# Finer first pieces, alternating and limited transfers, and rotary tables spread on chip, at the head of an encoder block

## The reference

```python
h = rms_norm(x, norm_gain[l])                       # over 2048 channels
proj = jnp.einsum('bsd,dc->bsc', h, w_in[l])        # to 11776 columns
qa, ka, va, ga, qb, kb, vb, gb, za, zb = jnp.split(proj, split_at, axis=-1)
# mixer A: 8 query heads, 2 key/value heads of 128, 2-D axial rotary over a grid of 64 columns
qa = axial_rotary(rms_norm(qa, q_norm_gain[l]), row_id, col_id)
ka = axial_rotary(rms_norm(ka, k_norm_gain[l]), row_id, col_id)
ya = grid_gqa_attention(qa, ka, va) * jax.nn.silu(ga)
# mixer B: 3 groups of 4 heads with dilated windows; then both branches are projected,
# gated by sigmoid(za), sigmoid(zb), merged, projected by w_out and added to x; final rms_norm
```

## Time and profile before

| what | value |
|---|---|
| time, median of 3 | 1177.59 us (1177.51 to 1177.87) |
| profiled execution | 1174.25 us |
| its span, slowest core (2) | 1172.4 us (cores: 1166.3 to 1172.4) |
| PE busy | 1125.9 us, 96% |
| DVE, ACT busy | 608.5, 507.4 us |
| moved by DMA | 102.18 MB |

### The profile page before, as it was taken

How to read it: one execution, slowest core, us unless ns; L and a number is a source line. 1 busy time by engine, 2 the same in 40 slices (tenths; PEclk the granted TensorE clock), 3 DMA queues, 4 the chain that set the end, 5 groups by cost and what they waited for, 6 DMA issues and landing times.

```text
span 1172.4 us, 17560 instructions; the slowest of 8 cores (1166.3 to 1172.4 us)
## 1 busy us (share of the span) xinstructions
PE 1125.9 (96%) x5844; PEld 556.0 (47%) x5956; DVE 608.5 (52%) x942; ACT 507.4 (43%) x907; POOL 79.2 (7%) x163
## 2 busy tenths in 40 slices
PE   3899999999999999999999999999999999999996
PEld 1655544444444544544554455444444444444443
DVE  2589878888886555663754654421212122122155
ACT  3465688888886444543543543411111111111232
POOL 0000000000000000000000000011111111010000
PEclk9999999999999999999999999999999999999999
DMA  9956512222232424333323420155656645449433
GB/s 221 261 183 158 106 19 37 37 37 37 37 73 38 89 37 72 55 55 55 57 53 55 70 36 1 19 95 89 117 88 115 103 69 87 70 93 247 129 144 144
DMA packets 30040, 102.18 MB, mean 87 GB/s; under 512 B 3456, under 2 KB 7552, under 8 KB 26880
## 3 DMA queue, kind: packets, MB, share of 16 engines
q0 software_dynamic: 20304, 63.27, 32.8%
q1 hardware_dynamic: 9648, 37.78, 9.6%
HBM read 155.90 MB, written 8.39 MB: 140 GB/s over the span
## 4 chain that ended last, share of the span: by engine, by line
PE 90%; DVE 3%; DMA 3%; issue 2%; ACT 1%; ACTq 0%; SPq 0%; DVEq 0%; POOLq 0%
PE pb L218 90%; DVE s_hT L218 2%; DVE s_arena L218 1%; DMA s_wsl<-w_in 1%; DMA s_yaT<-xt 1%; DMA s_rope<-ropeB 1%; ACT s_arena L218 1%; ACT s_rs L218 0%; DVE s_yaT L218 0%; ACT s_stat L218 0%; SPq L218 0%; DVEq L216 0%; ACTq L1439 0%; ACT s_gain L218 0%; ACTq L216 0%
## 5 line engine op out<-in xcount | busy, mean ns | idle before, releaser
L218 PE MATMUL pb<-s_hT,s_wsl 128*128 128x512 bf16 (+1 forms) x3445 | 747.8, 367 | 15.2 <-DVE s_hT L218 8.0
L218 PEld LDWEIGHTS pb<-s_hT,s_wsl 128*128 128x128 bf16 x3520 | 336.4, 98 | 377.2 <-issue 20.8
L218 ACT ACTIVATE s_arena<-pb 128x512 bf16<-128x512 f32 (+5 forms) x472 | 264.4, 575 | 266.3 <-PE pb L218 210.7
L218 DVE TENSOR_TENSOR s_arena<-pb,s_arena 128x512 f32<-128x512 f32 x112 | 88.9, 794 | 289.5 <-PE pb L218 283.0
L218 ACT ACTIVATE s_arena<-pb,s_mb 128x512 f32<-128x512 f32 x64 | 44.0, 687 | 250.3 <-PE pb L218 250.2
L218 PE MATMUL pb<-s_arena 128*128 128x512 bf16 (+3 forms) x692 | 134.7, 305 | 2.0 <-DVE s_arena L218 1.3
L218 DVE TENSOR_TENSOR s_arena<-s_arena 64x512 bf16<-64x512 f32 (+2 forms) x128 | 100.6, 786 | 21.7 <-ACT s_arena L218 14.7
L218 POOL DMA_DIRECT2D s_wsl<-w_in x92 | 48.7, 530 | 825.7 <-PE pb L218 775.8
L218 DVE TENSOR_TENSOR s_arena<-s_arena,s_rope 128x512 f32<-128x512 f32 (+3 forms) x136 | 89.8, 660 | 4.1 <-DVE s_arena L218 0.5
L218 PEld LDWEIGHTS pb<-s_arena 128*128 128x128 bf16 x704 | 59.8, 98 | 57.0 <-issue 1.8
L218 DVE TENSOR_TENSOR s_gain<-s_gain 128x512 f32<-128x512 f32 x96 | 66.3, 691 | 22.6 <-ACT s_gain L218 12.9
(11 more groups left out here) (71 smaller groups left out, 604.5 us busy)
## 6 DMA issues: line engine op xcount, KB each, us to landing
s_wsl<-w_in POOLq DMA_DIRECT2D x92, 512.0 KB, 5.2
y<-s_arena SPq DMA_DIRECT2D x14, 512.0 KB, 2.8
s_yaT<-xt SPq DMA_DIRECT2D x6, 1024.0 KB, 12.1
s_arena<-xt SPq DMA_DIRECT2D x4, 1024.0 KB, 25.1
s_wsl<-wba POOLq DMA_DIRECT2D x16, 256.0 KB, 3.7
s_hT<-xr SPq DMA_DIRECT2D x4, 1024.0 KB, 15.9
s_hT<-wout POOLq DMA_DIRECT2D x8, 512.0 KB, 33.9
s_ybT<-xt SPq DMA_DIRECT2D x2, 1024.0 KB, 21.8
```

What stands on the lines that cost most here:

```text
L218: ins = getattr(engine, fn[0])(**fn[1])
```

## The change

It has six parts. (1) The head units become 128, 128, 256, 256, 256, 512 and 512 tokens; the first two are one piece each. (2) The transfers of the start are issued as x0, w, x1, w, x2, w, x3, w, x4, x5, x6, x7, w, w, and each waits until the one four places ahead of it has landed. (3) The full rotary tables of mixer A (2 MB in four transfers) are replaced by one of 64 KB, since a value depends on the row or on the column of the token grid alone; six DVE copies and two ACT copies of 32 partitions x 2048 spread it into the same tables. (4) The small gain vectors go by POOL's queue, ahead of the weights, and ACT starts with a Ln on one column. (5) The planner's model of DMA becomes a flow on two queues with a share each, with other start times. (6) Six bonuses change (`silu_post` in mixer A and in mixer B, both from 0.3 to 0.1; `v_post`, `kq_post`, `attA_PV` and the projections). The diff, cut to its core:

```diff
-        self.te = {e: 0.0 for e in ENGS}
-        self.dma_free = 0.0
+        self.te = {e: 0.4 for e in ENGS}
+        self.te["sp"] = 1.0
+        self.dq = {"sp": [], "pool": []}
...
-        self.te[eng] = start + 0.06
+        self.te[eng] = start + (0.45 if eng == "sp" else 0.55)
...
-        self.dma_free = max(self.dma_free, start) + n / 300000.0
         ent[1] += 16
-        tok = (ent[0], ent[1], None, "d_" + semname, self.dma_free + 2.0)
...
+        self.dq[eng].append([self.te[eng], n, tok])
+        self.flow()
...
+            rate = {e: 290000.0 if len(act) == 1 else 290000.0 * (0.68 if e == "sp" else 0.32) for e in act}
...
+                qs[e1][pos[e1]][2][4] = now + 2.0
+                pos[e1] += 1
...
-    ropeA_d = din("ropeA", [2, 128, T])
+    ropeA_d = din("ropeA", [128, 2, 64])
...
+        HU = []
+        for n_ in (128, 128, 256, 256, 256, 512, 512):
+            g_ = HU[-1][0][-1] + 1 if HU else 0
+            HU.append((tuple(range(g_, g_ + n_ // 128)), 128 * g_, n_))
+        XN = [u_[2] for u_ in HU for g in u_[0]]
+        UEND = [u_[0][-1] + 1 for u_ in HU for g in u_[0]]
...
-        def xload(g):
-            S.dma("sp", XB[g], xt_d[g].rearrange("p (k n) -> p k n", k=XB[g].shape[1]), "x%d" % XBUF[g], writes=XK[g])
-
-        def rope_load(s):
-            sl = slice(512 * s, 512 * (s + 1))
-            S.dma("sp", rope[:, :, sl], ropeA_d.rearrange("a p t -> p a t")[:, :, sl], "c_rope%d" % s, writes=[rope_all[s]])
+        def xload(g, after=()):
+            S.dma("sp", XB[g], xt_d[g].rearrange("p (k n) -> p k n", k=XB[g].shape[1]), "x%d" % XBUF[g], reads=list(after), writes=XK[g])
+
+        def rope_tables():
+            for i in range(4):
+                p0 = 32 * i
+                out = rope[p0:p0 + 32].rearrange("p a (r c) -> p a r c", c=64)
+                if i % 2 == 0:
+                    src_ = rsm[p0:p0 + 32, :, 0:32].unsqueeze(3).to_broadcast([32, 2, 32, 64])
+                else:
+                    src_ = rsm[p0:p0 + 32].unsqueeze(2).to_broadcast([32, 2, 32, 64])
+                for a in range(2):
+                    if i == 3:
+                        ACT(out[:, a], src_[:, a], AF.Copy, ["rsm"], ["rope2"])
+                    else:
+                        CP(out[:, a], src_[:, a], ["rsm"], rope_all)
...
-        S.dma("sp", gnt[:], gn_d, "c_gnt", writes=["gnt"])
-        S.dma("sp", qkg[:], qkg_d, "c_qkg", writes=["qkg"])
...
         MEMSET(one_t[:], 1.0, ["one"], eng="dve")
-        for g in range(2):
-            xload(g)
-        w_issue()
-        w_issue(XK[0])
-        xload(2)
-        xload(3)
-        w_issue(XK[1])
-        w_issue(XK[1])
-        for g in range(4, 8):
-            xload(g)
-        rope_load(0)
-        rope_load(1)
-        w_issue(XK[7])
-        w_issue(XK[7])
+        ACT(stat[:, 0:1], one_t[:], AF.Ln, ["one"], ["pre"])
+        S.dma("pool", rsm[:], ropeA_d, "c_rsm", writes=["rsm"])
+        S.dma("pool", gnt[:], gn_d, "c_gnt", writes=["gnt"])
+        S.dma("pool", qkg[:], qkg_d, "c_qkg", writes=["qkg"])
+        gone = []
+        for it in ['x0', 'w', 'x1', 'w', 'x2', 'w', 'x3', 'w', 'x4', 'x5', 'x6', 'x7', 'w', 'w']:
+            after = gone[-4] if len(gone) >= 4 else ()
+            if it[0] == "x":
+                g_ = int(it[1:])
+                xload(g_, after)
+                gone.append(XK[g_])
+            else:
+                gone.append([("w", wslot_of(wstate["issued"]))])
+                w_issue(after)
+
+        rope_tables()
...
-        HU = [((2 * u, 2 * u + 1), 256 * u, 256) for u in range(4)] + [((8, 9, 10, 11), 1024, 512), ((12, 13, 14, 15), 1536, 512)]
...
-                    if g == 5 or g == 9:
-                        rope_load(2 if g == 5 else 3)
...
-                n = 256 if s < 2 else 512
-                for tt in range(0, 512, n):
+                for gs, u0, n in HU:
+                    if u0 // 512 != s:
+                        continue
+                    tt = u0 - t0
                     for q in range(4):
-                        yield from ge("sc", (4 * s + 2 * (tt // 256) + q // 2 + 1) if s < 2 else 4 * s + q + 1)
+                        yield from ge("sc", gs[min(len(gs) - 1, (4 * q + 3) * len(gs) // 16)] + 1)
...
-                yield from ge("sc", ch + 2 if ch < 8 else 4 * s + 4)
+                yield from ge("sc", UEND[ch])
...
-            return 0.3 if pj_n[0] < at_n[0] + 1.15 else 0.0
+            return 0.5 if pj_n[0] < at_n[0] + 1.15 else 0.0
...
-                                   lambda h=h: X.get("E_done") >= 2 * (h - 1), partial(X.setf, ("sg", h, sl))), 0.3, "silu")
+                                   lambda h=h: X.get("E_done") >= 2 * (h - 1), partial(X.setf, ("sg", h, sl))), 0.1, "silu")
...
-                            fork(v_post(b, t0, n_, n), 0.2, "vpost")
+                            fork(v_post(b, t0, n_, n), 0.1, "vpost")
...
-                            fork(kq_post(b, t0, n_, n, fam == "qb"), 0.4, "kqpost")
+                            fork(kq_post(b, t0, n_, n, fam == "qb"), 0.2, "kqpost")
...
-        X.spawn(attA_PV(), 0.03, "PV")
+        X.spawn(attA_PV(), 0.06, "PV")
```

More of the change, by code:

```diff
@@ L143, in dma, with flow @@
         return tok
+    def flow(self):
+        qs = {e: self.dq[e][-14:] for e in self.dq}
+        left = {e: [j[1] for j in qs[e]] for e in qs}
+        pos = {e: 0 for e in qs}
+        now = 0.0
+        while any(pos[e] < len(qs[e]) for e in qs):
+            heads = [e for e in qs if pos[e] < len(qs[e])]
+            act = [e for e in heads if qs[e][pos[e]][0] <= now]
+            later = [qs[e][pos[e]][0] for e in heads if qs[e][pos[e]][0] > now]
+            if not act:
+                now = min(later)
+                continue
+            rate = {e: 290000.0 if len(act) == 1 else 290000.0 * (0.68 if e == "sp" else 0.32) for e in act}
+            t, e1 = min((now + left[e][pos[e]] / rate[e], e) for e in act)
+            if later and min(later) < t:
+                t, e1 = min(later), None
+            for e in act:
+                left[e][pos[e]] -= rate[e] * (t - now)
+            now = t
+            if e1 is not None:
+                qs[e1][pos[e1]][2][4] = now + 2.0
+                pos[e1] += 1
     def alias(self, new_key, old_keys):
@@ L365, in build_nc @@
         mb = sb("s_mb", [128, 32], F32)
+        rsm = sb("s_rsm", [128, 2, 64], F32)
         eps_t = sb("s_eps_t", [128, 1], F32)
@@ L689, in v_proj @@
                 s, i, tc0 = ch // 4, ch // 2 % 2, 128 * ch
-                yield from ge("sc", ch + 2 if ch < 8 else 4 * s + 4)
+                yield from ge("sc", UEND[ch])
                 b = yield from X.alloc("pj", 1)
                 for c in range(2):
+                    yield from ge("sc", UEND[ch + c])
                     tc = tc0 + 128 * c
@@ L1458, in _rope_tables @@
     SA = np.concatenate([sr, sc, -sr, -sc], axis=1).T
+    small = np.zeros((128, 2, 64), np.float32)
+    for a, tab in enumerate((CA, SA)):
+        grid = tab.reshape(128, 32, 64)
+        for i in range(4):
+            p = slice(32 * i, 32 * i + 32)
+            small[p, a, :32 if i % 2 == 0 else 64] = grid[p, :, 0] if i % 2 == 0 else grid[p, 0, :]
     cb, sbb = angles(pos, 32, 500000.0)
@@ L1462, in _rope_tables @@
     SB = np.concatenate([-sbb, zero, sbb, zero], axis=1).T
-    return (np.ascontiguousarray(np.stack([CA, SA])).astype(np.float32),
+    return (small,
             np.ascontiguousarray(np.stack([CB, SB])).astype(np.float32))
@@ L1527 @@
         xc = x[b][tok]
-        m["xt"] = np.concatenate([
-            xc[:1024].reshape(4, 256, 2, 8, 128).transpose(0, 2, 4, 3, 1).reshape(8, 128, 2048),
-            xc[1024:].reshape(2, 512, 4, 4, 128).transpose(0, 2, 4, 3, 1).reshape(8, 128, 2048)])
+        pieces, t0 = [], 0
+        for n in (128, 128, 256, 256, 256, 512, 512):
+            kn = 2048 // n
+            pieces.append(xc[t0:t0 + n].reshape(n, 16 // kn, kn, 128).transpose(1, 3, 2, 0).reshape(16 // kn, 128, 2048))
+            t0 += n
+        m["xt"] = np.concatenate(pieces)
         m["xr"] = np.ascontiguousarray(xc[:TO])
```

20 lines of the change are left out of this document (11 added, 9 removed).

## The result

The changed kernel takes 1183.65 us (median of 6 runs, 1182.05 to 1186.67) against 1177.91 for the kernel before (6 runs of the same session, 1177.51 to 1179.77). The ratio is 1.0043, 95% interval 1.0031 to 1.0056: slower by 0.3 to 0.6%, outside the predicted range and on the side that I gave 0.14.

What follows compares the result with a forecast made beforehand. PE bounds the kernel, with more than half of its 46.5 idle us in the head. Head lead 4.3 us, bonuses zero, taken from the median 1177.6, gives 1173.3 us; range for 8 in 10, 1169.8 to 1178.8.

Steps and rivals of the forecast that it cites:

- the side that I gave 0.14: Whole kernel: the changed kernel would be slower than the kernel before by more than 0.2%; chance 0.14.
- The step that failed: All stages: the six changed bonuses only reorder the list and were costed at zero.
- The slower rival: Attention, 130 to 700 us: smaller `silu_post` bonus returns PSUM banks late on 24 posts, some 12 us lost, near 1181; chance 0.13.
- The head: First 60-odd us: earlier transfers remove PE's 3.2 us wait for Q weights and 1.7 us of low clock; lead 4.3 us.
- K's block of 60: Head: 60 K matmuls of 128 columns after piece 3's sum, starting about 30.3 and taking 6.6 us.
- The state: Head: all eight sums, K of 768 tokens, V of 512, half the first Q head: 61.0; 11 more K matmuls: 62.3.
- The packet rule: Head transfers: queues alternate by packet, so 1 KB-packet pieces beside Q weights get an eighth of the bytes; price 0 to 2 us.
- The size of the head's gain: Head: the followed state reached at 62.3 instead of 66.6, a lead of 4.3 us that lasts to the end.
- my first rival: Head: K waits for piece 3, landing at 31.3, so gain is 0 to 2 us, 1176 to 1178; chance 0.22.
- My second rival: Gain above 6 us: less clock drop, fast DVE copies, 2 us less idle at 700 to 900; 1169.5 to 1171.5; chance 0.17.

Runs made afterwards that it cites:

- after_again: The changed kernel unchanged, measured again in another session against the kernel before: 1179.87 us against 1176.35, ratio 1.0031.
- old_bonuses: The changed kernel with all six bonuses put back to their old values, against the kernel before: 1170.67 us against 1174.58, ratio 0.9966.
- run 5: The changed kernel unchanged, measured again in another session, the same run as after_again: ratio 1.0031 to the kernel before.
- Runs 1 and 2: First the changed kernel with the six old bonuses, ratio 0.9966; second the kernel before with only the six new bonuses, ratio 1.0113.
- runs 3, 4 and 6: The changed kernel with old bonuses put back for PV only (1183.55 us), for K/Q and V only (1171.18 us), and for all three (1170.67 us).
- run 6, kq_pv_back: The changed kernel with K/Q, V and PV bonuses put back, `silu` and projection bonuses left new: 1170.67 us, ratio 0.9943 to the kernel before.
- run 1: The changed kernel with all six bonuses put back, the same run as old_bonuses: 1170.67 us, ratio 0.9966 to the kernel before.
- old_units: old_bonuses with head units of 256, 256, 256, 256, 512, 512 tokens again: 1170.54 us, ratio 0.994 to the kernel before.

## Why the prediction was wrong, step by step

**The step that failed** is the last one: "The bonuses change no work, only order. I cost them at zero." They cost, by stage and median core of after_again against before, 4.6 us at 180 to 340, 4.1 at 450 to 640 and 1.6 at 640 to 720, and 2.2 come back at 720 to 800 (in old_bonuses too, so this is not the bonuses' doing). With 0.6 at 340 to 450 and -1.4 in the head that is +7.3, and the median spans are 7.4 apart. By the ratio of run 5 the time itself moved by some 3.6 us: the slowest cores of before are those with a clock drop in the head, and its one profile is of a quick execution (1174.25 against a median of 1177.91). So the stages say where the time went, and not how much of it to the microsecond. Runs 1 and 2 show the cause both ways, runs 3, 4 and 6 divide its stages between PV's bonus and those of K/Q and V. "No work, only order" is true and no reason for zero: PE takes its list in order, and the list had just enough projections between the dependent matmuls to cover DVE. In the sum's terms: this term was put at 0. Between old_bonuses and the second measurement of after the ratios are 0.0065 apart, 7.6 us, and the stages from 180 to 800 add up to 10.0. All the rest of the change, forecast at -4.3, came to a ratio of 0.9966, -4.0.

**The slower rival** had the right kind of place and a wrong part. Its condition, idle of PE from 130 to 700 up by more than 6.7, was met: 4.6 + 0.6 + 4.1 + 1.6 = 10.9 by the table, and 2.9 + 5.1 = 8.0 by the waits alone on core 1. But it accused `silu_post` and PSUM banks on 24 posts, and run 6 acquits that bonus. What waits is PE for an operand from DVE, not for a bank. I had priced one of the six numbers and not asked the same of the other five.

**The head** came out near its own steps, with terms off that cancel:
- The first Q head's weights land at 43.9 and the wait is gone, as forecast; K's block of 60 starts at 31.0 (30.3 forecast).
- The second weight block was to land at 17 or 18; issued at about 3.8, it was under way for 19.9 us and landed near 24. Three small transfers now stand ahead of the weights on POOL's queue, and the first block took 15.0 us, where it took 10.1 before; no run puts these three back by themselves. Piece 3's sum was waited for longer, so nothing hung on it.
- The row of 64 matmuls at 31.00 is 60 of 128 columns and 4 of 256. The 60 take 5.3 us, not 6.6: 39 of them 4.0 us at a granted clock of 0.50 (0.10 each), the other 21 some 1.3 at 1.00 (0.06 each), below the 0.098 of the weight load that I had taken as the lower bound. The 16 scalings of 128 tokens 4.29 us, 0.27 each, not 0.34; the DVE copies 1.30 each (7.82 / 6), not 1.9 to 2.8. But the 64 KB landed only at 9.9 (8.3 us under way), not at 4, so ACT's two copies stand in front of the first Square, 13.86. K waits for piece 3 anyway.
- The scaling of unit 3 starts at 50.63 (51.5 forecast) and takes 6.42 us; the earlier trace rows had the same 6.42 for tokens in the arena, and I took 16 x 0.477 = 7.6 from pieces in hT. The state comes at 60.35 (61.0).

**The packet rule.** From 40 to 42 us, with Q weights beside a piece in hT, the queues of core 5 show:

```profile
q0 software_dynamic: 68, 0.28, 82.6%
q1 hardware_dynamic: 65, 0.06, 14.2%
```

Equal counts, a fifth of the bytes: the starving that I described is there. Its price is at the low end of the 0 to 2 us given. The wait of 1.43 ahead of the sum at 51.28 is not it: piece 6, issued at 31.08, landed 17.0 us later at 48.1, and its Square started at 49.23, behind two operations for `s_rs`. The sum of piece 7, at 56.48, has no wait at all. The Trainium skill, page "DMA: Bandwidth & Descriptors", section on queues, rings and completion order, has each engine take its queues in turn by packet; by that rule, the trace agrees.

**The size of the head's gain** is the term that was mis-sized, and its near agreement with run 1 (3.9 against 4.3) is partly luck. I read the stall and the low clock on core 2. Of the eight cores of before, only 0, 2 and 6 have the clock at 0.5 (1.2 GHz) at 58 to 61 us; they reach the mark at 228.0 to 228.5, the other five at 223.1 to 224.9. In old_bonuses all eight reach it at 221.8 to 224.6. So the head gives 4 to 6 us on the cores with the drop and about 1 on the others, 1.4 at the median. That is within the 0 to 2 of my first rival, but not for its reason: piece 3 came nearly when I had it (its Square starts at 27.29, and I had 26.5 for the landing). The other 2.3 of old_bonuses' gain come from 720 to 800, where its list hardly waits. My second rival named those 2 us, as a thing on top. Some are taken back at 340 to 450, where cores 2 and 4 of old_bonuses have a low clock near 349 that before has not.

**What stays open:** why PE's order at 720 to 800 differs between lists. The trace shows the order and the wait, but no run changed that place alone. Nor did a run take one `kq_post` or `v_post` bonus by itself, or part (4) back alone, and nothing shows what brings the stretches at 0.81.

**The better version.** kq_pv_back and old_units (1170.67 and 1170.54, ratios 0.9943 and 0.994) beat both kernels; with old_bonuses that is 0.3 to 0.6% under before.

## What to carry to other kernels

Where a list is written at build time, a number that only sorts it is an edit of every stage, and is priced at the thinnest cover in each: here PE had at most 0.8 us idle in 170, which meant that there was nothing to win and 4 to 5 us to lose in each of two stages. Test such numbers by themselves, apart from the change that they come with. And before a stall of one core is put into a sum, look at how many cores have it, since the time is that of the slowest and the next may be only 1 us behind.

## What the runs showed of the hardware

- A granted clock of 0.81, neither of the two levels otherwise seen, for about 15 us at a time, two or three times, on all cores of one die in one profile of the fourteen. A weight load takes 0.11 us there (6.70 / 62 in the window above) and not 0.098.
- What a small transfer at the start takes hangs on where it stands: on POOL's queue, behind two 1 MB pieces that SP had begun to issue, 64 KB issued at 1.57 us took 8.3 us, 8 KB behind it 9.0 and 1 KB 9.2. In the kernel before, SP issued the same 8 KB and 1 KB itself, and they took 1.6 and 2.4.
- With a new weight tile each, matmuls of 128 columns start every 0.10 us at a granted clock of 0.50 and every 0.06 at 1.00, though a weight load shows 0.098.
- A wait of PE shown as 0.3 us costs about 0.17 more: seven waits of 2.3 us in all and one of 0.6 come to 4.6 us lost in mixer A, and 2.9 + 8 x 0.17 is 4.3.
